# Six rounded weight slots moved to the top of SBUF, 32 bytes past a multiple of 64

## The reference

```
def rmsnorm(x, g): return x * rsqrt(mean(x*x) + EPS) * g
for i in range(2):
    xn = rmsnorm(x, g_mix[i])
    if i == 0:   # mLSTM: q, k, v, o and gates from one projection, then the output projection
        p = xn @ a_w_in            # 1024 x 3080
        y = (norm(mlstm(p)) * a_g_out * sigmoid(o)) @ a_w_out   # 1024 x 1024
    else:        # chunk MLP
        u, v = split(gelu(xn @ b_w_in))        # 1024 x 4096
        y = (u * (tril(w_s) @ layernorm(v) + b_s)) @ b_w_out    # 2048 x 1024
    x = x + y
    g, up = split(rmsnorm(x, g_ffn[i]) @ f_w_gu[i])             # 1024 x 5632
    x = x + (silu(g) * up) @ f_w_down[i]                        # 2816 x 1024
y = rmsnorm(x, g_final)
```

## Time and profile before

| | |
|---|---|
| median of 3 runs | 2795.29 us (2789.36 to 2796.79) |
| profiled execution | 2791.7 us |
| its span, first to last instruction | 2789.9 us |
| TensorE matmuls, busy | 2763.6 us, 99%, 18522 instructions |
| TensorE weight loads, busy | 2720.0 us, 97% |
| VectorE / ScalarE / GpSimd, busy | 1518.3 / 736.5 / 1116.8 us |
| mean granted TensorE clock | 0.998 of full speed |

### The profile page before, as it was taken

The page is one execution under the profiler, slowest core; times in us unless marked ns, Lnnn a source line. Parts: engine busy times, 40 slices in busy tenths (PEclk is TensorE's granted clock), DMA queues, the critical chain, the costliest instruction groups (busy, mean ns, idle before and its releaser), DMA issues.

```text
span 2789.9 us, 48475 instructions
## 1 busy us (share of the span) xinstructions
PE 2763.6 (99%) x18522; PEld 2720.0 (97%) x18522; DVE 1518.3 (54%) x2886; ACT 736.5 (26%) x1482; POOL 1116.8 (40%) x731
## 2 busy tenths in 40 slices
PE   9999999999999999999999999999999999999999
PEld 7898989899999999999999999999999999999998
DVE  4545372886555555556511565700575555555557
ACT  5302020452222222223311311300432222222224
POOL 4232224135444444444334143344244444444441
PEclk9999999999999999999999999999999999999999
DMA  3321212111111111111111111111111111111112
GB/s 107 89 70 43 68 48 71 40 39 46 45 45 45 45 45 45 45 45 53 32 46 39 54 54 38 39 53 38 46 31 46 45 45 45 45 45 45 45 46 87
DMA packets 188209, 139.39 MB, mean 50 GB/s; under 512 B 6899, under 2 KB 176715, under 8 KB 188108
## 3 DMA queue, kind: packets, MB, share of 16 engines
q1 hardware_dynamic: 188108, 137.96, 16.7%
HBM read 127.32 MB, written 10.62 MB: 49 GB/s over the span
## 4 chain that ended last, share of the span: by engine, by line
PE 88%; DVE 7%; ACT 3%; issue 1%; POOL 0%; DMA 0%; DVEq 0%; ACTq 0%; SPq 0%; POOLq 0%
PE ps L1274 33%; PE ps L923 22%; PE ps L1331 18%; PE ps L1406 7%; PE ps L1096 4%; PE ps L1468 1%; DVE xn_lo L2101 1%; DVE xs_lo L2464 1%; DVE p_lo L2707 1%; PE ps L1514 1%; PE ps L1216 1%; DVE state L2301 0%; ACT xs_hi L1721 0%; DVE xT L2447 0%; PE ps L1233 0%
## 5 line engine op out<-in xcount | busy, mean ns | idle before, releaser
L1274 PE MATMUL ps<-xs_hi,w_hi 128*128 128x288 f32 x2496 | 739.6, 296 | 0.4 <-issue 0.4
L1274 PE MATMUL ps<-xs_lo,w_hi 128*128 128x288 f32 x2496 | 736.2, 295 | 0.0
L1274 PE MATMUL ps<-xs_hi,w_lo 128*128 128x288 f32 x2496 | 734.0, 294 | 0.0
L846 POOL TENSOR_TENSOR w_lo<-w_raw,w_hi 128x512 fp32r<-128x512 f32 x304 | 403.4, 1329 | 580.7 <-ACT w_hi L1709 580.7
L820 POOL TENSOR_TENSOR w_hi<-w_raw,ones 128x1024 fp32r<-128x1024 f32 x80 | 196.6, 2458 | 773.5 <-PE ps L923 531.6
L1274 PEld LDWEIGHTS ps<-xs_hi,w_lo 128*128 128x128 f32 x2496 | 470.1, 188 | 0.0
L1274 PEld LDWEIGHTS ps<-xs_hi,w_hi 128*128 128x128 f32 x2496 | 467.7, 187 | 1.3 <-issue 1.1
L1274 PEld LDWEIGHTS ps<-xs_lo,w_hi 128*128 128x128 f32 x2496 | 468.6, 188 | 0.3
L1709 ACT ACTIVATE w_hi<-w_raw 128x512 fp32r<-128x512 f32 x304 | 189.9, 629 | 785.4 <-PE ps L1274 248.4
L2447 DVE TENSOR_TENSOR xT<-xT,ps 128x384 f32<-128x384 f32 x528 | 286.3, 552 | 192.5 <-PE ps L1331 186.5
L1331 PE MATMUL ps<-hg_hi,w_hi 128*128 128x384 f32 x1008 | 337.0, 334 | 3.1 <-DVE hg_lo L2439 3.1
(11 more groups left out here) (332 smaller groups left out, 4965.6 us busy)
## 6 DMA issues: line engine op xcount, KB each, us to landing
w_raw<-in_f_w_gu_dram SPq DMA_DIRECT2D x88, 512.0 KB, 3.8
w_raw<-in_f_w_down_dram SPq DMA_DIRECT2D x44, 512.0 KB, 3.5
w_raw<-in_b_w_in_dram SPq DMA_DIRECT2D x32, 512.0 KB, 3.8
w_raw<-in_a_w_in_dram SPq DMA_DIRECT2D x24, 512.0 KB, 4.3
w_raw<-in_b_w_out_dram SPq DMA_DIRECT2D x16, 512.0 KB, 3.6
out_dram<-y_out SPq DMA_DIRECT2D x9, 512.0 KB
x_in<-in_x_prompt_dram SPq DMA_DIRECT2D x8, 512.0 KB, 5.8
c_nat<-in_state_C_dram SPq DMA_DIRECT2D x8, 512.0 KB, 8.7
```

The source lines that it names most:

```text
L846: nc.gpsimd.tensor_tensor(left(layer, w_lo, pos), src, left(layer, w_hi, pos).bitcast(F32), ALU.subtract).then_inc(left_lo, 1)
L1274: ins = pe.matmul(out, left(layer, w, pos)[:, k, :], r[:, s, x, k, :], start=(first and k == 0 and m == 0), stop=(last_one and k == KH - 1 ...
```

## The change

The six slots are no longer allocated behind `w_raw`. They are allocated in the group that holds `eps_t`, behind it. `ident` to `tri_s` and all stage buffers thereby move down by 6 x 4096 = 24576 bytes, which is 384 x 64, so each keeps its distance from a multiple of 64. `eps_t` is at 204736 (3199 x 64), takes 4 bytes, and the first slot starts at the next multiple of 32, 204768 = 3199 x 64 + 32. The other five follow at distances of 4096. The last slot ends at 229344. No instruction, semaphore, DMA or order is changed.

```diff
         w_raw = [sb(f"w_raw{r}", [P, KD, P]) for r in range(2)]
-        w_hi = [sb(f"w_hi{s}", [P, KD, P], F32R) for s in range(3)]
-        w_lo = [sb(f"w_lo{s}", [P, KD, P], F32R) for s in range(3)]
         ident = sb("ident", [P, P])
...
         with ExitStack() as part:
-            sb("below_eps", [P, STAGE_WORDS], F32, part)
+            sb("below_weights", [P, STAGE_WORDS], F32, part)
             eps_t = sb("eps_t", [P, 1], F32, part)
+            w_hi = [sb(f"w_hi{s}", [P, KD, P], F32R, part) for s in range(3)]
+            w_lo = [sb(f"w_lo{s}", [P, KD, P], F32R, part) for s in range(3)]
```

## The result

The changed kernel takes 2777.12 us (median of 4 runs, 2775.93 to 2778.48); before, in the runs made beside it, 2793.28 us (2789.36 to 2796.79). The ratio is 0.9943, with a 95% interval of 0.993 to 0.9955. It is faster by 16 us. I forecast 2795 with a range from 2784 and gave "faster" a chance of 0.11. The forecast was wrong.

A forecast was written before the change was run, and what follows sets the result against it. The prediction took TensorE's matmul stream, count times start-to-start distance, as the bound. Its terms, 0 + 0 + 0 + 0, left the profiled 2791.7 us, given as 2795 near the median of 2795.3; range 2784 to 2825.

The forecast's parts named there:

- What bounds the kernel: Whole kernel: a stream of TensorE matmuls, its time their number times the start-to-start distance; 2532 us, 91% of the span.
- The slot as stationary operand: 14,544 matmuls at L1274, L1331 and L923: weight loads starting 32 bytes past cost 0, upper bound 25 us.
- The doubt: The plain float32 matmuls used as evidence are spaced 429 ns apart, not 133, so they may hide more load time.
- The slot as moving operand: 2592 matmuls at L1406 and L1096: reading 32 bytes past costs 0, bound 10 us, no gain allowed.
- outer bounds of 58 and 10 us: 4 ns, taken from 382 against 378 ns, on each of 14,544 stationary-slot and 2592 moving-slot matmuls.
- Writers and everything else: ScalarE and GpSimd writing displaced slots, GpSimd reading them back, and stage buffers and constants moved by multiples of 64: 0.
- Rival A: L1274, L1331, L923: the 13.3 ns surplus is unhidden weight load and grows; 25 us slower, 2820; chance 0.20.
- counterargument from L960: L960 loads only 8 columns, in 88 ns instead of 188, yet its matmuls keep a surplus of 15 ns.
- Rival B: L1406 and L1096: displaced moving reads cost more, up to 10 us, 2805 at the most; chance 0.06.
- Rival C: All 17,136 rounded matmuls: operand reads collide in a 64-byte stretch, displacement frees them; up to 183 us faster, 2612; chance 0.12.
- a tenth of it: 2777: A tenth of the 183 us gain from freeing colliding operand reads, giving a time of 2777 us.
- What would show it: Trace signs: 133.3, 120.0 and 173.3 ns kept if right; wrong if any moves by more than half a nanosecond.

The follow-up runs named there:

- the sweep: Kernel without the computation: groups of 64 matmuls with chosen columns, type and stationary/moving displacement in bytes (0/0, 32/0); float32r at 256 columns took 120.0 and 118.3 ns.

## Why the prediction was wrong

- **What bounds the kernel**: right. Three distances times their counts is the time, and the gain is the change in two of them, 16.6 us by the distances and 16.2 by the medians. That one nanosecond on all slot-reading matmuls is 17 us was the right warning.
- **The slot as stationary operand, value 0**: failed. The step took L1190 and L1233 for the nearest rows. They are plain float32, at two cycles a column, and the sweep has 2.5 ns of surplus for this kind both at 0/0 and at 32/0. They were near in address and far in what decides. The doubt was written down ("hide more"), and then the value was set as if it had been answered. Measured: 1.07 ns less at L1274, 0 at L1331 and L923.
- **The slot as moving operand, value 0 and "below zero I give nothing"**: failed on the same ground, with the earlier trace rows. The row was also read for more than it holds: 378 and 382 ns were taken for a price of a displacement by 4 bytes, and the outer bounds of 58 and 10 us were built on it. But the first pair of L1210, which moves the aligned row 0 of `v_tok`, has 382 and 380 ns in the same trace, and all 64 matmuls of L1216 lie between 377 and 382. Measured: 3.33 ns less on 2592 matmuls, half of the gain. No reason stood there that excluded a gain, so the lower end should not have been closed.
- **Writers and everything else, 0**: right.
- **Rival A** (unhidden load): refuted, as its own counterargument from L960 said; with 8 columns the surplus is 14.5 ns. The two figures that the prediction took from the Trainium skill (TensorE: Matmul & The Clock Gate, Weight-path perf modes) are not stated there for float32r: the 32 cycles are theory for fp8 weights, and the line of 16 bytes stands with a loading mode for fp8. **Rival B** (displaced moving read): the sign was wrong at L1406, which ran 3.33 ns faster.
- **Rival C** (collision of the two operands' reads): the right family, with a chance of 0.12. Its "a tenth of it: 2777" is the measured time, by luck of a round fraction. What spoke against it was again a row of another kind (L1190) and L960, which excludes a dependence on the length of the load but not on the meeting of two streams. With no other engine at work, moving the slots against the activations changes the distance by up to 6.7 ns. C's own picture, two reads in one 64-byte stretch, does not hold as it stood: 64 bytes of displacement change the distances too, and so does a shift of both operands by 16. The Trainium skill (TensorE: Matmul & The Clock Gate, Step-by-step: what each phase is for) gives the two operands a read port each, from which I had concluded that C was impossible. The runs do not show whether the ports are shared, but they contradict the conclusion: where the two operands lie against each other changed the time.
- **The range**: A and B got 30 us above, C 11 below. Two unknown mechanisms of the same size deserved the same room, and 2777 would have been inside.
- **What would show it**: the sign was read right ("the prediction is wrong if any of the three distances moves by more than half a nanosecond"), and it let the place of the gain be found in one view.

What stays open: by what mechanism the two operands' addresses act together. That their reads collide is the natural guess, and no run shows it. The runs show that the distance depends on the addresses of both operands and on the order of reads, that it does not repeat after 64 bytes (whether after 128 was not tested), and that one set of addresses can have more than one repeating pattern. They show it for float32r and exclude it for plain float32 at 256 columns; bfloat16 was not tested where float32r reacts. The surplus of 13.3 ns itself was never removed: 6.7 at 256 columns was the lowest.

## What to carry to other kernels

Where TensorE streams float32r without a gap, measure the distance from start to start against columns / 2.4: of a surplus of 13 ns or so, a part depends on where the operands lie against each other. A small kernel that repeats only the order of addresses shows it in one run, if it keeps the true differences between addresses and not their remainders. Check such a layout in the kernel itself, because at some addresses what runs before picks a slower pattern. And bound an unseen cost from rows of the same type and rate, or leave both ends open.

## What the runs showed of the hardware

- float32r: columns + 13.3 ns when the tiles of both operands start alike, at a multiple of 64 or 32 past one (slots 64 bytes on: 132.2 instead of 133.3 ns at 288 columns). With both 16 past it was 131.1 ns for 288 columns, 175.6 for 384 and 118.3 for 256.
- bfloat16 (162.5 ns for 384 columns) and float32 (215.9 for 256 at two cycles): columns + 2.5 ns, at 0/0 and with the stationary operand 32 past.
- At 256 columns the surplus of float32r was 13.3, 11.7, 10.0 and 6.7 ns at different displacements; at 384 it was 13.3 to 17.7, at 512 it was 13.3 or 20.0.
- A shift of both operands by 32 bytes changed nothing at relative 0 and +32; one by 16 did.
- With the slots 16 past, two patterns were seen at the same addresses, 173.3 and 176.7 ns, picked by what ran before, in the sweep and in the loop of a whole kernel.
